# In three of a transformer kernel's linear layers, an input's high and low parts become one 512-column operand

## The chip, the cores and the metric

The kernel runs on one core of a Trainium2 chip. The metric is the device time of one execution, in microseconds (us). The version before takes 1366.85 us, the median of three runs (1366.1 to 1367.48).

## What is computed

The reference chains two transformer-like parts over 256 tokens of width 1024. The first has a mixer (pooling, indexed sparse attention, gates) and a convolved feed-forward layer. The second has two layers with a context stream of another 256 tokens. Cut to the three layers that the change touches:

```python
def hybrid_mixer(...):
    ...
    return merged @ w_out                      # "w_out": 1024 -> 1024

def conv_ffn(xn, w_up, conv_w, conv_b, w_down):
    ...
    return (jax.nn.silu(a) * b) @ w_down       # "w_down": 2816 -> 1024

def _mlp(h, w1, w2):
    return jnp.square(jax.nn.relu(h @ w1)) @ w2   # its last call: "w2_1", 4096 -> 1024
```

Each result is added to the running activation: h + hybrid_mixer(...), h + conv_ffn(...), and x + gx2 * _mlp(...). The whole is in float32.

## The kernel before

**Layout.** Features lie on the partitions and tokens along the columns. R holds the activation as 8 chunks of 128 features by 512 columns, tokens of x on the left (0 to 255), tokens of the context on the right.

**Precision.** A float32 product is made of float32r products of split operands. A weight is split into whi and wlo, an input into a high and a low part (Ahi and Alo, Hhi and Hlo, Zhi and Zlo). The product is whi·high + whi·low + wlo·high, all three summed in one PSUM bank.

**Blocks, units, chunks.** A weight matrix is cut into blocks of 128 x 128; 8 blocks are a unit, one DMA of 512 KB into one of 9 raw buffers. ScalarE writes whi for a unit (line 1000, 4 buffers), VectorE writes wlo over the raw buffer (line 1463). A chunk is one output tile of 128 features, summed over kt blocks: kt is 8 in w_out (8 chunks, 64 blocks), 22 in w_down (8 chunks, 176 blocks), 32 in w2_1 (8 chunks, 256 blocks). For a layer with only the tokens of x, a block costs three matmuls of 256 columns: whi with the high part (line 508), whi with the low part (line 520), wlo with the high part (line 522). Layers that also have the context do the same with 512 columns. The chunks take turns in three PSUM banks of 512 columns; of these the 256-column layers use the left half.

**First chunk of a layer with kt of 8.** Where n is 0 and the layer is not in EARLY, linear does the high parts of the eight blocks with whi and wlo (lines 508 and 511) first, and then the eight low parts (line 515), because the inputs are still being made. Of the three layers this is so in w_out alone.

**Reading.** VectorE adds a finished chunk to R: line 1714 in w_out, line 1780 in w_down, line 1857 (gated) in w2_1. The reading is queued between the wlo operations in the order that walk gives.

**What sets the order.** The order of units is PLAN, written out by weight_plan. In w_out and in w_up it places two units of another matrix (raw<-in_ada, eight matmuls at line 563) behind every second unit. SP's queue loads unit i when unit i-9 has been used. Each engine walks the same plan in a hand-written order. Waits are on semaphores; Waits.wait_ge leaves out one already met.

**Work around the change.** After w_out's chunks, ScalarE makes the input of w_up (line 1011) and squares of R (line 1015). TensorE sums the squares after w_up's first chunk (lines 611 and 613). In w_down, ScalarE and GpSimd sum the squares of the context (lines 1015 and 2094), and TensorE takes the sum after unit 4 (lines 611 and 613, called from after_down). After w_down's last chunk come two squares of R (line 1015), their sums over partitions on TensorE (lines 611 and 613), a reciprocal (line 1792), a root, and then ab_in's inputs. Its weights' first unit is loaded when w_down's unit 19 has been used, and its whi and wlo stand ahead of w_down's last reading in the queues of ScalarE and VectorE. w2_1 is the last layer: SP writes chunk c of R out (line 477) when VectorE has read it.

Of the kernel before, what the change touches and what calls it, by code (L numbers as in the profile page):

```python
# [262 lines left out]
def launch_program(nc, dram, out):  # L263
# [19 lines left out]
    R = sb("R", 8 * 512).rearrange("p (c t) -> p c t", c=8)  # L283
    Ahi = sb("Ahi", 8 * 512, f32r).rearrange("p (c t) -> p c t", c=8)
    Alo = sb("Alo", 8 * 512, f32r).rearrange("p (c t) -> p c t", c=8)
    h_at = here[0]
    here[0] += 65536
    Hhi = sb("Hhi", 8192, f32r, at=h_at)
    Hlo = sb("Hlo", 8192, f32r, at=h_at + 32768)
    par = sb("par", N_PARAMS)  # L290
# [45 lines left out]
    def h32(name, cols, at):  # L336
# [18 lines left out]
    z2 = h32("z2", 2048, 38912).rearrange("p (c t) -> p c t", c=8)  # L355
    Zhi, Zlo = [sb(f"Z{x}", 1024, f32r, at=h_at + 47104 + 4096 * i).rearrange("p (c t) -> p c t", c=4)
                for i, x in enumerate(("hi", "lo"))]
    F = h32("F", 2048, 0).rearrange("p (c t) -> p c t", c=4)
# [122 lines left out]
    def tensor_program(e):  # L481
        w = Waits(e)
        bank6 = [None]

        def linear(name, T, acts, hi_ready, lo_ready, during=None, following=None, midway=None, begin=0):


            kt, nt = WEIGHTS[name]
            for n in range(begin, nt):
# [6 lines left out]
                for k in range(kt):  # L496
# [9 lines left out]
                    w.wait_ge(S("whi"), s + 1)  # L506
                    hi_ready(k)
                    e.matmul(o, w_hi, ah, start=k == 0, stop=False)  # L508
                    if kt == 8 and n == 0 and name not in EARLY:
                        low_ready(s)  # L510
                        e.matmul(o, w_lo, ah, start=False, stop=False)
                        if last:
                            for x in range(8):
                                lo_ready(x)
                                m = e.matmul(o, whi[s % NHI][:, 128 * x:128 * x + 128], acts(x)[1][:, :Tn],
                                             start=False, stop=x == 7)
                            m.then_inc(S("mm").sem, 1)
# [255 lines left out]
        linear("w_pool", 256, lambda k: (Ahi[:, 4 + k], Alo[:, 4 + k]), ready("mix_hi"), ready("mix_lo"))  # L773
        linear("w_out", 256, z_parts, ready("Z_hi"), ready("Z_lo"), following=lambda u: ada_following("w_out", u))

# [12 lines left out]

        linear("w_down", 256, lambda k: Hc(k, 256), ready("H_hi"), ready("H_lo"), following=after_down)
        row_sum(ps[5][:, :256], ssum[:, :256], sq[0][:, :256], "nx_part", 6, "nx_sq", 8, "nx_sum")  # L790
# [195 lines left out]
        linear("w1_1", 258, lambda k: (Ehi[:, k], Elo[:, k]), e2_hi, e2_lo, during=during_1)  # L986
        linear("w2_1", 256, lambda k: Hc(k, 256), ready("h1_hi"), ready("h1_lo"))

# [465 lines left out]
    def vector_program(e):  # L1454
# [251 lines left out]
        for what, i in walk("w_out"):  # L1706
            if what == "unit":
                los(UNIT["w_out", i])
            if what == "chunk":
                if i:  # L1710
                    early_lo("e1", E_hi, E_lo, i - 1, LEFT, param("g_ffn", i - 1))
                o = product("w_out", i)[:, :256]

                e.scalar_tensor_tensor(R[:, i, LEFT], o, 0.5, R[:, i, LEFT], MUL, ADD).then_inc(S("wout_r").sem, 1)
                if i == 7:
                    w.wait_ge(S("wout_r"), 8)
                    early_lo("e1", E_hi, E_lo, 7, LEFT, param("g_ffn", 7))
# [57 lines left out]
        for what, i in walk("w_down"):  # L1775
            if what == "unit":
                los(UNIT["w_down", i])
            if what == "chunk":
                o = product("w_down", i)[:, :256]
                e.tensor_tensor(R[:, i, LEFT], o, R[:, i, LEFT], ADD).then_inc(S("down_r").sem, 1)  # L1780
            if what == "after":
# [288 lines left out]
        for what, i in walk("w2_1"):  # L2070
            if what == "unit":
                los(UNIT["w2_1", i])
            if what == "chunk":
                gated("w2_1", "d1_r", 1, 1, i, 256, None)

# [330 lines left out]
```

## Time and profile before

| | |
|---|---|
| median of 3 runs | 1366.85 us |
| profiled execution, its own time | 1367.44 us |
| its span, first to last instruction | 1365.2 us |
| granted TensorE clock over the span | 0.995 |
| w_out, TensorE, about | 191.9 to 220.5 us |
| w_down, TensorE | 356.7 to 422.4 us |
| w2_1, TensorE | 1270.1 to 1362.4 us |

A row of a timeline has its start from the beginning of the span, its duration and its instruction. Matmuls are pipelined, so one lasts longer in the rows than the distance between the starts of two: the distance is what a matmul costs in a stream. PE is TensorE's matmuls, PEld its weight loads, DVE VectorE, ACT ScalarE, POOL GpSimd, SPq the DMA queue of SyncE.

### The profile page before, as it was taken

The page shows a single profiled execution, that of the slowest core. Times are in us where ns is not written, and L with a number is a line of the kernel's source. Part 1 is how long each engine was busy: PE and PEld are TensorE (multiplying, and loading weights), DVE is VectorE, ACT ScalarE, POOL GpSimd, SP SyncE. Part 2 cuts the span into 40 slices and gives each one's busy share as a digit, 9 for nine tenths or more (in the row PEclk, how much of TensorE's full clock was granted, in tenths as well). Part 3 has the DMA queues.
Part 4 walks back from the last instruction along what each step waited for, and adds up shares of the span by engine and source line. Part 5 has one row for each costly group of instructions (what it writes and reads, how often), then busy time and mean ns, then how long its engine had stood idle before and what let it go on. Part 6 is the DMA issues. An engine that isn't in the chain of part 4 may idle for free.

```text
span 1365.2 us, 20841 instructions
## 1 busy us (share of the span) xinstructions
PE 1330.2 (97%) x8320; PEld 1141.9 (84%) x8320; DVE 810.3 (59%) x1223; ACT 594.2 (44%) x952; POOL 429.6 (31%) x439
## 2 busy tenths in 40 slices
PE   6999999999999999989999999999899999999999
PEld 6888898899997788858878888887577777999999
DVE  6678576899776452386633444343667765855443
ACT  4336545566664132244421244222545544666432
POOL 3443221222420003244400044111466552388200
PEclk9999999999999999999999999999999999999999
DMA  6777457865556231344534444444523221555552
GB/s 256 261 252 270 139 175 275 296 204 184 181 172 207 69 96 59 97 166 156 168 127 156 150 139 146 142 144 159 181 93 108 94 93 32 188 184 185 184 185 78
DMA packets 63967, 220.13 MB, mean 161 GB/s; under 512 B 6912, under 2 KB 10240, under 8 KB 63872
## 3 DMA queue, kind: packets, MB, share of 16 engines
q1 hardware_dynamic: 63584, 218.56, 47.9%
q8 instruction: 66, 1.08, 0.3%
q10 hardware_dynamic: 288, 0.25, 0.1%
q14 instruction: 29, 0.24, 0.1%
HBM read 217.73 MB, written 1.05 MB: 160 GB/s over the span
## 4 chain that ended last, share of the span: by engine, by line
PE 89%; DVE 6%; issue 2%; POOL 1%; ACT 1%; DMA 1%; DVEq 0%; ACTq 0%; POOLq 0%
PE ps L508 26%; PE ps L522 25%; PE ps L520 25%; PE ps L563 2%; PE ps L882 1%; DVE wlo L1463 1%; PE ps L909 1%; PE ps L896 1%; PE ps L828 1%; DVE Alo L1886 1%; DVE tmp L1901 1%; PE ps L875 1%; POOL ssum_c L2094 1%; DVE tmp L1728 1%; PE ps L807 0%
## 5 line engine op out<-in xcount | busy, mean ns | idle before, releaser
L508 PE MATMUL ps<-Ahi,whi 128*128 128x256 f32 (+2 forms) x1640 | 541.4, 330 | 8.3 <-ACT Ahi L1025 5.5
L522 PE MATMUL ps<-Ahi,wlo 128*128 128x256 f32 (+2 forms) x1596 | 510.2, 320 | 0.7 <-DVE wlo L1463 0.6
L520 PE MATMUL ps<-Alo,whi 128*128 128x256 f32 (+2 forms) x1596 | 509.8, 319 | 0.0
L1463 DVE TENSOR_TENSOR wlo<-raw,whi 128x1024 fp32r<-128x1024 f32 x305 | 388.2, 1277 | 104.0 <-ACT whi L1000 104.0
L1000 ACT ACTIVATE whi<-raw 128x1024 fp32r<-128x1024 f32 x305 | 320.1, 1051 | 284.4 <-PE ps L522 220.3
L508 PEld LDWEIGHTS ps<-Ahi,whi 128*128 128x128 f32 x1640 | 312.6, 191 | 73.4 <-issue 30.8
L522 PEld LDWEIGHTS ps<-Ahi,wlo 128*128 128x128 f32 x1596 | 304.5, 191 | 22.7 <-DVE wlo L1463 1.6
L520 PEld LDWEIGHTS ps<-Alo,whi 128*128 128x128 f32 x1596 | 304.5, 191 | 22.4 <-issue 1.7
L520 PE MATMUL ps<-Hlo,whi 128*128 128x256 f32 (+1 forms) x728 | 233.8, 321 | 0.0
L508 PE MATMUL ps<-Hhi,whi 128*128 128x256 f32 (+1 forms) x688 | 222.5, 323 | 0.0
L522 PE MATMUL ps<-Hhi,wlo 128*128 128x256 f32 (+1 forms) x688 | 221.9, 322 | 0.0
L520 PEld LDWEIGHTS ps<-Hlo,whi 128*128 128x128 f32 x728 | 139.3, 191 | 10.0
L2083 POOL TENSOR_TENSOR Hlo<-tmp,Hhi 128x256 fp32r<-128x256 f32 (+1 forms) x86 | 121.5, 1413 | 62.7 <-ACT Hhi L1295 40.8
L508 PEld LDWEIGHTS ps<-Hhi,whi 128*128 128x128 f32 x688 | 131.0, 190 | 11.6 <-issue 0.8
L522 PEld LDWEIGHTS ps<-Hhi,wlo 128*128 128x128 f32 x688 | 131.0, 190 | 10.0
L1857 DVE SCALAR_TENSOR_TENSOR R<-ps,ada,R 128x256 f32<-128x256 f32 x64 | 28.7, 480 | 156.0 <-PE ps L522 151.9
L2211 POOL TENSOR_TENSOR tmp<-tmp 128x512 f32<-128x512 f32 (+1 forms) x64 | 54.4, 850 | 166.3 <-ACT tmp L1290 166.3
L2094 POOL TENSOR_TENSOR ssum<-ssum,sq 128x256 f32<-128x256 f32 (+1 forms) x30 | 31.8, 1059 | 166.4 <-ACT sq L1015 166.4
L1541 DVE SCALAR_TENSOR_TENSOR modsum<-raw,cond,modsum 128x1024 f32<-128x1024 f32 x36 | 62.0, 1739 | 0.0
L1290 ACT ACTIVATE tmp<-ps 128x512 f32<-128x512 f32 x32 | 19.2, 599 | 97.5 <-PE ps L522 90.8
L1295 ACT ACTIVATE Hhi<-tmp 128x512 fp32r<-128x512 f32 (+1 forms) x64 | 33.7, 526 | 35.6 <-POOL tmp L2211 35.4
L2225 POOL TENSOR_TENSOR tmp<-tmp,tmp 128x512 f32<-128x512 f32 (+1 forms) x32 | 33.8, 1056 | 44.9 <-ACT tmp L1348 43.6
(263 smaller groups left out, 1286.0 us busy)
## 6 DMA issues: line engine op xcount, KB each, us to landing
raw<-in_ada SPq DMA_DIRECT2D x96, 512.0 KB, 4.3
raw<-in_w SPq DMA_DIRECT2D x64, 512.0 KB, 3.5
raw<-in_w_up SPq DMA_DIRECT2D x44, 512.0 KB, 3.9
raw<-in_w_in SPq DMA_DIRECT2D x38, 512.0 KB, 5.1
raw<-in_w_0a SPq DMA_DIRECT2D x32, 512.0 KB, 3.6
raw<-in_w_0b SPq DMA_DIRECT2D x32, 512.0 KB, 3.5
raw<-in_na_in SPq DMA_DIRECT2D x24, 512.0 KB, 5.6
raw<-in_w_down SPq DMA_DIRECT2D x22, 512.0 KB, 3.5
```

The costliest lines, as they stand in the source:

```text
L508: e.matmul(o, w_hi, ah, start=k == 0, stop=False)
L520: e.matmul(o, w_hi, al, start=False, stop=False)
L522: m = e.matmul(o, w_lo, ah, start=False, stop=last)
L1000: e.activation(whi[s % NHI][:, :cols], raw[i % NRAW][:, :cols], ACT.Copy).then_inc(S("whi").sem, 1)
L1295: e.activation(Hc(n, T)[0], tmp[n % 5][:, :T], ACT.Copy).then_inc(S(st + "_hi").sem, 1)
L1463: e.tensor_tensor(wlo[i % NRAW][:, :cols], raw[i % NRAW][:, :cols], plain(whi[s % NHI][:, :cols]), SUB).then_inc(S("wlo").sem, 1)
L1541: d = e.scalar_tensor_tensor(total, raw[i % NRAW], cond[:, k, v:v + 1], total, MUL, ADD)
L1857: e.scalar_tensor_tensor(R[:, n, half(q)], o[:, half(q)], gate, R[:, n, half(q)], MUL, ADD).then_inc(S(made).sem, 1)
L2083: e.tensor_tensor(into, x, plain(hi), SUB).then_inc(S(done).sem, 1)
L2094: e.tensor_tensor(total, total, x, ADD).then_inc(S(st + "_part").sem, 1)
L2211: e.tensor_tensor(x, x, x, MUL).then_inc(S(st + "_sq").sem, 1)
L2225: e.tensor_tensor(m, m, r, MUL).then_inc(own.sem, own.up())
```

## The change

In the three layers the high and the low part of an input are put into one tile each (A, H and Z), so that one access pattern (A2, H2, Z2) gives 256 columns of the high part and 256 of the low part of a chunk. whi then meets both in one matmul of 512 columns, which fills the whole bank: whi·high on the left and whi·low on the right. wlo·high is added on the left, as before. The wait for the low part stands ahead of this matmul. VectorE adds the left half of the bank to R and then, after a wait for that, the right half. The first chunk of w_out keeps its order and puts the low parts' sum on the right.

```diff
-    Ahi = sb("Ahi", 8 * 512, f32r).rearrange("p (c t) -> p c t", c=8)
-    Alo = sb("Alo", 8 * 512, f32r).rearrange("p (c t) -> p c t", c=8)
+    A = sb("A", 2 * 8 * 512, f32r).rearrange("p (x c t) -> p x c t", x=2, c=8)
+    Ahi, Alo, A2 = A[:, 0], A[:, 1], A.rearrange("p x c t -> p c x t")[:, :, :, 0:256]
...
-    Hhi = sb("Hhi", 8192, f32r, at=h_at)
-    Hlo = sb("Hlo", 8192, f32r, at=h_at + 32768)
+    H = sb("H", 2 * 8192, f32r, at=h_at)
+    Hhi, Hlo, H2 = H[:, 0:8192], H[:, 8192:16384], H.rearrange("p (x c t) -> p c x t", x=2, t=256)
...
-    Zhi, Zlo = [sb(f"Z{x}", 1024, f32r, at=h_at + 47104 + 4096 * i).rearrange("p (c t) -> p c t", c=4)
-                for i, x in enumerate(("hi", "lo"))]
+    Z = sb("Z", 2 * 1024, f32r, at=h_at + 47104).rearrange("p (x c t) -> p x c t", x=2, c=4)
+    Zhi, Zlo, Z2 = Z[:, 0], Z[:, 1], Z.rearrange("p x c t -> p c x t")
...
                     hi_ready(k)
+                    if both and not (kt == 8 and n == 0):
+                        lo_ready(k)
+                        e.matmul(ps[g % 3].rearrange("p (x t) -> p x t", x=2), w_hi, both(k), start=k == 0, stop=False)
+                        low_ready(s)
+                        m = e.matmul(o, w_lo, ah, start=False, stop=last)
+                        if last or end:
+                            m.then_inc(S("mm").sem, 1)
...
+                        continue
                     e.matmul(o, w_hi, ah, start=k == 0, stop=False)
...
-                                m = e.matmul(o, whi[s % NHI][:, 128 * x:128 * x + 128], acts(x)[1][:, :Tn],
-                                             start=False, stop=x == 7)
+                                m = e.matmul(ps[g % 3][:, 256:512] if both else o, whi[s % NHI][:, 128 * x:128 * x + 128],
+                                             acts(x)[1][:, :Tn], start=False, stop=x == 7)
...
-        linear("w_out", 256, z_parts, ready("Z_hi"), ready("Z_lo"), following=lambda u: ada_following("w_out", u))
+        linear("w_out", 256, z_parts, ready("Z_hi"), ready("Z_lo"), following=lambda u: ada_following("w_out", u),
+               both=lambda k: A2[:, k] if k < 4 else Z2[:, k - 4])
...
-        linear("w_down", 256, lambda k: Hc(k, 256), ready("H_hi"), ready("H_lo"), following=after_down)
+        linear("w_down", 256, lambda k: Hc(k, 256), ready("H_hi"), ready("H_lo"), following=after_down, both=lambda k: H2[:, k])
...
-        linear("w2_1", 256, lambda k: Hc(k, 256), ready("h1_hi"), ready("h1_lo"))
+        linear("w2_1", 256, lambda k: Hc(k, 256), ready("h1_hi"), ready("h1_lo"), both=lambda k: H2[:, k])
...
-                o = product("w_out", i)[:, :256]
-
-                e.scalar_tensor_tensor(R[:, i, LEFT], o, 0.5, R[:, i, LEFT], MUL, ADD).then_inc(S("wout_r").sem, 1)
+                o = product("w_out", i)
+
+                e.scalar_tensor_tensor(R[:, i, LEFT], o[:, LEFT], 0.5, R[:, i, LEFT], MUL, ADD).then_inc(own.sem, own.up())
+                w.wait_ge(own, own.n)
+                e.scalar_tensor_tensor(R[:, i, LEFT], o[:, RIGHT], 0.5, R[:, i, LEFT], MUL, ADD).then_inc(S("wout_r").sem, 1)
```

The readings of w_down (tensor_tensor) and w2_1 (scalar_tensor_tensor with the gate, in place of the call of gated) are doubled in the same way, with the wait between the two halves.

## Rows read from the trace of the kernel before

**Rows 1.** The page: span, busy time of each engine, the chain that ended last.

```profile
span 1365.2 us, 20841 instructions
...
PE 1330.2 (97%) x8320; PEld 1141.9 (84%) x8320; DVE 810.3 (59%) x1223; ACT 594.2 (44%) x952; POOL 429.6 (31%) x439
...
PE 89%; DVE 6%; issue 2%; POOL 1%; ACT 1%; DMA 1%; DVEq 0%; ACTq 0%; POOLq 0%
```

**Rows 2.** Busy time of each engine, granted clock and DMA by stretch.

```profile
core 0: us, PE busy (x) PEld busy (x) DVE busy (x) ACT busy (x) POOL busy (x), PEclk, DMA share, GB/s
1270.00:1362.00 92.00, 92.00 (x770) 92.00 (x769) 39.17 (x39) 31.92 (x32) 3.29 (x4) 1.00 0.47 150
604.00:685.00 81.00, 81.00 (x358) 66.88 (x357) 52.81 (x36) 31.89 (x44) 39.24 (x30) 1.00 0.48 163
373.00:416.00 43.00, 43.00 (x358) 42.95 (x357) 27.88 (x38) 23.44 (x36) 9.77 (x11) 1.00 0.55 175
196.00:222.00 26.00, 25.52 (x206) 21.62 (x206) 15.11 (x22) 14.11 (x24) 5.00 (x7) 1.00 0.76 266
```

**Rows 3.** Timeline, w2_1: its first matmul and its last instructions.

```profile
1270.09 0.28 PE L508 MATMUL ps<-Hhi,whi 128*128 128x256 f32 x1
...
1362.11 0.28 PE L522 MATMUL ps<-Hhi,wlo 128*128 128x256 f32 x1
1362.43 0.48 DVE L1857 SCALAR_TENSOR_TENSOR R<-ps,ada,R 128x256 f32<-128x256 f32 x1 [8.77 <-PE ps L522]
1362.94 0.33 SPq L477 DMA_DIRECT2D out_y<-R  x1
```

**Rows 4.** Timeline, a stream of 512-column matmuls, its first and last.

```profile
604.10 0.39 PE L508 MATMUL ps<-Ahi,whi 128*128 128x512 f32 x1
...
684.82 0.39 PE L522 MATMUL ps<-Ahi,wlo 128*128 128x512 f32 x1
```

**Rows 5.** Timeline, weight loads beside matmuls, 512 columns and 256 columns.

```profile
700.31 0.39 PE L520 MATMUL ps<-Hlo,whi 128*128 128x512 f32 x1
700.54 0.39 PE L522 MATMUL ps<-Hhi,wlo 128*128 128x512 f32 x1
...
700.31 0.19 PEld L522 LDWEIGHTS ps<-Hhi,wlo 128*128 128x128 f32 x1
...
1361.87 0.28 PE L508 MATMUL ps<-Hhi,whi 128*128 128x256 f32 x1
1361.87 0.19 PEld L520 LDWEIGHTS ps<-Hlo,whi 128*128 128x128 f32 x1
1361.99 0.28 PE L520 MATMUL ps<-Hlo,whi 128*128 128x256 f32 x1
```

**Rows 6.** Timeline, w_down: its first matmul, and around the sum after unit 4.

```profile
356.67 0.28 PE L508 MATMUL ps<-Hhi,whi 128*128 128x256 f32 x1
...
370.95 0.28 PE L522 MATMUL ps<-Hhi,wlo 128*128 128x256 f32 x1
372.45 0.70 PE L611 MATMUL ps<-ssum_c,con 128*128 128x256 f32 x2 [1.22 <-POOL ssum_c L2094]
372.99 0.59 PE L613 MATMUL ps<-X,con 128*128 128x256 f32 x2
373.23 0.47 PE L508 MATMUL ps<-Hhi,whi 128*128 128x256 f32 x1
```

**Rows 7.** GpSimd in w_down: its last Hlo (timeline), the sum of squares (the chain).

```profile
361.81 0.75 POOL L2083 TENSOR_TENSOR Hlo<-tmp,Hhi 128x256 fp32r<-128x256 f32 x1 [0.59 <-ACT Hhi L1165]
...
364.26 1.36 POOL ssum_c L2094
...
365.75 1.55 POOL ssum_c L2094
...
369.11 0.75 POOL ssum_c L2094
...
370.88 1.53 POOL ssum_c L2094
```

**Rows 8.** The end of w_down: TensorE's last matmul (timeline), the chain that ended last.

```profile
422.25 0.28 PE L522 MATMUL ps<-Hhi,wlo 128*128 128x256 f32 x1
...
416.81 3.45 DMA raw<-in_ab_in
...
420.28 1.07 ACT whi L1000
...
421.37 1.22 DVE wlo L1463
422.59 0.41 DVE R L1780
...
423.03 0.42 ACT sq L1015
...
423.50 0.70 PE ps L613 x2
```

**Rows 9.** Timeline, VectorE, two pairs of operations with a wait of its own between.

```profile
358.41 0.48 DVE L1728 SCALAR_TENSOR_TENSOR tmp<-Y,par,tmp 128x255 f32<-128x255 f32 x1 [0.74 <-ACT tmp L1187]
358.93 0.48 DVE L1730 SCALAR_TENSOR_TENSOR tmp<-Y,par,tmp 128x254 f32<-128x254 f32 x1
...
425.18 0.42 DVE L1790 SCALAR_TENSOR_TENSOR X<-ps,X 128x256 f32<-128x256 f32 x1 [0.52 <-PE ps L613]
425.63 1.75 DVE L1792 RECIPROCAL X<-X 128x256 f32<-128x256 f32 x1
```

**Rows 10.** Timeline, the end of w_out: ScalarE, and TensorE's sum after w_up's first chunk.

```profile
221.41 0.51 ACT L1011 ACTIVATE Ahi<-R,par 128x256 fp32r<-128x256 f32 x1 [0.58 <-DVE R L1714]
221.83 1.04 ACT L1000 ACTIVATE whi<-raw 128x1024 fp32r<-128x1024 f32 x1
222.78 0.40 ACT L1015 ACTIVATE sq<-R 128x256 f32<-128x256 f32 x1
...
224.48 0.59 PE L611 MATMUL ps<-ssum,con 128*128 128x256 f32 x2
224.91 0.59 PE L613 MATMUL ps<-sq,con 128*128 128x256 f32 x2
```

**Rows 11.** Timeline, VectorE: four pieces of 256 columns, against one run of 1024.

```profile
5.38 1.22 DVE L1553 TENSOR_TENSOR squares<-R 128x1024 f32<-128x1024 f32 x1 [5.38 <-DMA R<-in_x]
...
421.37 1.22 DVE L1463 TENSOR_TENSOR wlo<-raw,whi 128x1024 fp32r<-128x1024 f32 x1 [5.16 <-ACT whi L1000]
```

More of the change, by code:

```diff
@@ L483, in tensor_program, with linear @@
         bank6 = [None]
-        def linear(name, T, acts, hi_ready, lo_ready, during=None, following=None, midway=None, begin=0):
+        def linear(name, T, acts, hi_ready, lo_ready, during=None, following=None, midway=None, begin=0,
+                   both=None):
             kt, nt = WEIGHTS[name]
@@ L507, in linear @@
                     hi_ready(k)
+                    if both and not (kt == 8 and n == 0):
[5 more added lines that the diff above has]
+                            m.then_inc(S("mm").sem, 1)
+                        if last and during:
+                            during(n)
+                        if end and following:
+                            following(blk // 8)
+                        continue
                     e.matmul(o, w_hi, ah, start=k == 0, stop=False)
@@ L1778, in vector_program @@
             if what == "chunk":
-                o = product("w_down", i)[:, :256]
-                e.tensor_tensor(R[:, i, LEFT], o, R[:, i, LEFT], ADD).then_inc(S("down_r").sem, 1)
+                o = product("w_down", i)
+                e.tensor_tensor(R[:, i, LEFT], o[:, LEFT], R[:, i, LEFT], ADD).then_inc(own.sem, own.up())
+                w.wait_ge(own, own.n)
+                e.tensor_tensor(R[:, i, LEFT], o[:, RIGHT], R[:, i, LEFT], ADD).then_inc(S("down_r").sem, 1)
             if what == "after":
@@ L2073, in vector_program @@
             if what == "chunk":
-                gated("w2_1", "d1_r", 1, 1, i, 256, None)
+                o, gate = product("w2_1", i), ada[:, 1, 0, 40 + i:41 + i]
+                e.scalar_tensor_tensor(R[:, i, LEFT], o[:, LEFT], gate, R[:, i, LEFT], MUL, ADD).then_inc(own.sem, own.up())
+                w.wait_ge(own, own.n)
+                e.scalar_tensor_tensor(R[:, i, LEFT], o[:, RIGHT], gate, R[:, i, LEFT], MUL, ADD).then_inc(S("d1_r").sem, 1)
     def gpsimd_program(e):
```

## The prediction

> **What bounds the kernel now.** I read the page first [rows 1]. TensorE's matmuls are busy for 1330.2 of 1365.2 us and carry 89% of the chain that ended last, so a saving counts only if it shortens TensorE's own stream, or a wait between its matmuls. The table by stretch [rows 2] shows that in all three layers TensorE is busy almost without a gap at the full granted clock (1.00, 2.4 GHz), VectorE for 39.17 of 92 us in w2_1 and 27.88 of 43 in w_down, and the DMA for 0.47 to 0.76 of the time. So the question is what one matmul costs inside a stream.
>
> That is the distance between starts, not the duration in a row. w2_1 has 8 x 32 x 3 = 768 matmuls of 256 columns; from the first to the last start [rows 3] are 92.02 us and 767 steps, **119.97 ns each**. The 512-column stream [rows 4] goes from the second block of a chunk to the last of w1_0a, 119 blocks of three, 80.72 us over 356 steps, **226.74 ns each**. The difference, 106.8 ns for 256 columns, is 2.4 columns per ns. Each matmul thus pays some 13.3 ns above its columns, at either width. It pays with every matmul, so fewer and wider ones are cheaper.
>
> **TensorE's part.** A block was three narrow matmuls, 3 x 119.97 = 359.9 ns. It becomes one wide and one narrow, 226.74 + 119.97 = 346.7 ns: 13.2 ns less. No row has the two widths taking turns, so the pair's cost is put together. The weight loads support it: the load for the next matmul starts when the one before it starts, at both widths [rows 5]. In the new stream the load that belongs to the next wide matmul can start with the narrow one and has its 120 ns as now, and the other load has 227. The blocks concerned are 56 in w_out (its first chunk keeps its order), 176 in w_down and 256 in w2_1, 488 in all. Raw savings: 56 x 13.2 = 0.74, 176 x 13.2 = 2.33, 256 x 13.2 = 3.39; 6.46 us.
>
> Here the Trainium skill (TensorE: Matmul & The Clock Gate, "Back-to-back issue gap") gives N / 2.4 + 2.5 ns for a warm stream. By that the estimate would be 2.5 ns saved per block, 1.2 us in all. The two rows say 13.3 at either width, and the sum goes by them.
>
> The wide operand is two pieces of 256 columns, 16 or 32 KB apart in the partition. TensorE reads no such operand in a row. The nearest row is VectorE's: four pieces of R take 1.22 us, like one run of 1024 columns [rows 11]. I take nothing for the jump. As bounds: a restart could cost as much as one matmul's excess, 13.3 ns, and more if it stalls; on the other side, the excess of the narrow matmul might vanish beside a wide one, another 13.3 saved.
>
> **Where it is lost.** In w_down TensorE waits after unit 4 for GpSimd's sum of the context's squares [rows 6]. It had the 40 blocks done at 356.67 + 40 x 0.36 = 371.07 and went on at 372.45. GpSimd's chain [rows 7] is tied to the end of w_up, not to w_down, so the 40 blocks' 0.53 us only lengthen this wait. GpSimd's operations last 0.75 us alone and 1.4 to 1.55 beside VectorE's; the doubled reading of chunk 0 moves a wlo operation by half a us there, which may hurt or help by up to 0.8 us. I take 0.
>
> At the end of w_down, the load of ab_in's first unit starts when unit 19 is done (416.81), then come whi, wlo, and only then VectorE's last reading at 422.59 [rows 8]. TensorE's last product is ready at about the same moment: its last matmul begins at 422.25 [rows 8], and readings start 0.32 after that, as 1362.11 and 1362.43 show [rows 3]. The two chains are now level. The last 16 blocks' 0.21 us are therefore lost to the load. 176 - 40 - 16 = 120 blocks are left, 1.59 us.
>
> **What VectorE adds.** Two operations with a wait between them start 0.52 apart where one lasts 0.48, and 0.45 where it lasts 0.42 [rows 9]. Within a layer this is hidden: a chunk's reading has two more chunks of TensorE's work before its bank is wanted, and VectorE has room. Eight more readings of 0.52 in w2_1 are 4.2 us against 53 idle [rows 2]; w_out's VectorE is busy for 15.11 of 26 us and takes 3.7 more. At a layer's end it shows:
> - w_out: the last chunk's input for w_up is ready at 221.92 and its square at 223.18; the sum wants it at 224.9 [rows 10]. TensorE is 0.74 earlier and the reading 0.45 later relative to it. Cover 1.7 us, used 0.45: nothing.
> - w_down: the reading stands on the chain to ScalarE's squares and the sums [rows 8]: 0.45 us. What is late next is ab_in's input, by the same.
> - w2_1: the last reading precedes the last output transfer [rows 3]: 0.52 us.
>
> **Waits, queues, memory.** The low part is now awaited one matmul sooner. In w_down GpSimd's last Hlo (block 21) is made by 362.6 [rows 7] and wanted at 356.67 + 21 x 0.35 = 364.0; in w2_1 block 31 comes 10.7 us after the first. Behind this wait stands only TensorE's own stream. No DMA is added or moved. SP's loads are freed by TensorE's progress and come 4% closer together, 266 to some 275 GB/s in w_out, at a DMA share of 0.76 now. The tiles occupy the same room.
>
> **The sum.** 0.74 + (1.59 - 0.45) + (3.39 - 0.52) = **4.75 us**. The profiled execution took 1367.44 us, 2.2 more than its span and 0.6 more than the median; the difference is taken from the median: 1366.85 - 4.75 = **1362.1 us**, 0.35% less.
>
> **The rivals.**
> 1. *The jump costs a restart.* If a second piece of an operand costs what a second matmul does, the wide one takes 240 ns and a block is unchanged. Only the two tails remain: 1366.85 + 0.97 = 1367.8 us, no change. For it: no row of TensorE excludes it. Against it: VectorE's equal times [rows 11]. Chance 0.10.
> 2. *The jump stalls, slower than before.* Its place is the wide matmul in 488 blocks. It decides from 17 ns per jump: (17 - 13.2) x 488 = 1.8 us, with the tails 2.8. At twice the excess, 26.6 ns, 6.5 + 0.97 us are added, 1374.3 us. For it speaks nothing in the rows, against it the same row as above. Chance 0.06. Here the Trainium skill (PSUM — Partial Sum Buffer, "Specifications (TRN2)") says that any non-contiguous access pattern slows matmuls significantly, without a figure. In the bank the halves lie side by side, so it would have to hold for the operand read; no row shows it.
> 3. *The narrow matmul's excess is its weight load.* The narrow stream has its loads busy for 92.00 of 92 us, the wide one for 66.88 of 81 [rows 2]. If a load could begin during the wide matmul for both of its successors, a block would save up to 26.5 ns. The 432 blocks that count would give 5.7 us more, 1356.4 us. Against it: the load starts with the matmul just before its own [rows 5]. Chance 0.05.
> 4. *The excess is mostly not per matmul.* If only 2.5 ns are saved per block, 432 x 2.5 = 1.1 us meet tails of 0.97 us: 1366.7 us. The two rows' equal excess speaks against it. Chance 0.04. That is the Trainium skill's gap rule from above, which the trace does not bear out.
> 5. *The change does not do what it says*, for one if the two pieces were fetched as two matmuls: the number of matmuls would stay 8320, and the time with it. It comes out as rival 1 and is counted there.
>
> **How the numbers follow.** My forecast has 0.75; its own range, by GpSimd's 0.8 us either way and a jump of up to 3 ns (1.3 us), is 1361 to 1364.5. The range leaves out rival 2, rival 1's full price and most of rival 3 (together under 0.2), takes in rival 4 and half the restart's price, and is 1360.2 to 1366.8. A measurement of this kernel can tell about 0.2%, 2.7 us, from no change. Faster by more than that: forecast and rival 3, 0.80. Within it: rivals 1 and 4 and little else, 0.14. Slower: rival 2, 0.06.
>
> **What would show it.** TensorE has 488 matmuls fewer, 7832. In w2_1, 512 starts span 256 x 0.3467 = 88.8 us, against 92.0. A wide matmul's start to the next is 227 ns, a narrow one's 120. The wait for GpSimd after unit 4 grows from 1.22 us to about 1.75. The last sum of w_down still follows a chain from the load of ab_in, with two readings of 0.42. The last output transfer starts about 1.0 us after the last product. The forecast is wrong if wide matmuls are more than 230 ns apart, if the narrow ones fall under 115, or if new waits for wlo stand in TensorE's stream.

## The result and the profile after

The changed kernel takes 1364.24 us in the median of 20 runs (1361.73 to 1366.55), the kernel before 1366.49 us in 20 runs beside it (1364.81 to 1367.99). The ratio is **0.9985, 95% interval 0.9978 to 0.9992**: 2.25 us faster, between 1.1 and 3.0. The direction is as forecast and the time lies in the range; the gain is half of the 4.75 us of the sum. The profiled execution took 1364.33 us.

The page after, for [rows 1]:

```profile
span 1362.1 us, 19938 instructions
...
PE 1325.6 (97%) x7832; PEld 1114.5 (82%) x7832; DVE 821.2 (60%) x1247; ACT 594.1 (44%) x952; POOL 428.5 (31%) x439
...
PE 88%; DVE 7%; issue 2%; DMA 1%; ACT 1%; POOL 1%; DVEq 0%; ACTq 0%; SPq 0%; POOLq 0%
```

488 matmuls are gone, as forecast, and TensorE still carries the chain. The table by stretch, for [rows 2]: w2_1, then w_down behind its fifth unit.

```profile
core 0: us, PE busy (x) PEld busy (x) DVE busy (x) ACT busy (x) POOL busy (x), PEclk, DMA share, GB/s
1268.00:1358.00 90.00, 90.00 (x512) 78.11 (x511) 42.56 (x46) 31.87 (x32) 3.33 (x4) 1.00 0.46 152
373.00:414.00 41.00, 41.00 (x238) 35.86 (x237) 30.09 (x44) 23.04 (x35) 8.55 (x11) 1.00 0.55 175
```

TensorE is still busy without a gap, at the full clock. w2_1 needs 90 us for its 512 matmuls where 88.8 were forecast. The start of each layer's first `wlo` matmul shows where the time went (us, before and after, shift; each from the timeline):

```
w_out, its second chunk    196.96    196.14   -0.82
w_up, first chunk          221.84    220.55   -1.29
w_down, first chunk        356.91    355.97   -0.94
w_down, end of unit 4      370.95    369.75   -1.20
w_down, end of unit 19     416.49    414.24   -2.25
w_down, last matmul        422.25    419.79   -2.46
ab_in                      429.45    427.49   -1.96
w2_1, first chunk         1270.32   1268.36   -1.96
w2_1, last matmul         1362.11   1358.46   -3.65
last transfer of out_y    1362.94   1359.80   -3.14
```

The first 0.82 us are not the change's: they arise before w_out's second chunk, where both kernels have the same matmuls. Until 160 us the profile of before was 0.67 us ahead; in the next 12 us, in which it has a lower granted clock, it fell back by 1.49. Before, then after:

```profile
160.00:172.00 12.00, 10.02 (x67) 9.45 (x66) 6.35 (x10) 6.46 (x13) 3.15 (x4) 0.86 0.46 133
```

```profile
160.00:172.00 12.00, 10.02 (x80) 9.44 (x79) 7.12 (x13) 7.08 (x14) 3.15 (x4) 1.00 0.41 138
```

From there on the sum of the prediction and the trace compare as follows (gains positive):

```
                              forecast   measured
w_out                            0.74       0.47
wait at w_up's first chunk       0         -0.35
w_down, to the end of unit 19    1.59       1.31
from there to ab_in             -0.45      -0.29
w2_1                             3.39       1.69
last reading                    -0.52      -0.51
sum                              4.75       2.32
```

2.32 us from one pair of traces, 2.25 from the medians. (The last 16 blocks of w_down, behind unit 19, gained another 0.21 us, and ab_in's load took them back, as forecast.) Two terms are well off, w2_1 and the wait in w_up; w_out and w_down are off by less. Each can be seen.

**w2_1: the rhythm.** The timeline of TensorE in w2_1 after:

```profile
1299.56 0.40 PE L513 MATMUL ps<-H,whi 128*128 128x512 f32 x1
1299.80 0.28 PE L515 MATMUL ps<-H,wlo 128*128 128x256 f32 x1
1299.92 0.40 PE L513 MATMUL ps<-H,whi 128*128 128x512 f32 x1
...
1300.62 0.40 PE L513 MATMUL ps<-H,whi 128*128 128x512 f32 x1
```

And in w_down, behind the wait after unit 4:

```profile
379.69 0.39 PE L513 MATMUL ps<-H,whi 128*128 128x512 f32 x1
...
380.73 0.40 PE L513 MATMUL ps<-H,whi 128*128 128x512 f32 x1
```

Three blocks take 1.06 us in the first and 1.04 us in the second. The trace's nanoseconds show two patterns. In the first the distances (wide to narrow plus narrow to wide) repeat every three blocks: 242+119, 236+114, 232+117 ns. In the second they repeat every two: 231+113, 232+117. Over long stretches a block takes **353.3 ns** in the first (w2_1, 90.10 us for 255 blocks from its first `wlo` matmul to its last) and **346.7 ns** in the second (w_down, 41.26 us for the 119 from unit 5 to unit 19); the expectations below call them 353.6 and 346.5. The forecast was 346.7, and before the change it was 360.0 (91.79 us in w2_1). All of w2_1 and the first five units of w_down run in the longer rhythm, the rest of w_down in the shorter one.

**w_up: a new wait.** TensorE at the end of w_up's first chunk, after:

```profile
222.82 0.28 PE L523 MATMUL ps<-A,whi 128*128 128x256 f32 x1
223.20 0.39 PE L535 MATMUL ps<-A,whi 128*128 128x256 f32 x1
```

VectorE at that place:

```profile
221.13 0.42 DVE L1730 SCALAR_TENSOR_TENSOR R<-ps,R 128x256 f32<-128x256 f32 x1
221.58 0.42 DVE L1732 SCALAR_TENSOR_TENSOR R<-ps,R 128x256 f32<-128x256 f32 x1
222.66 0.49 DVE L1492 SCALAR_TENSOR_TENSOR A<-R,par,A 128x256 fp32r<-128x256 f32 x1 [0.66 <-ACT A L1027]
```

The low part of w_up's last input (L1492) lasts from 222.66 to 223.15. TensorE wanted it at 222.94, 0.12 behind the start before, and started at 223.20; its next matmul (223.42) came 0.22 behind that one instead of 0.12. Together that is 0.36 us.

Before the change the same low part was ready at 222.53 and wanted at 224.24, 1.7 us of room; now it is 0.2 us late. Both traces show where the 1.9 us went. ScalarE makes the whi of w_up's first unit when its load has landed, before and after:

```profile
214.34 1.06 ACT L1000 ACTIVATE whi<-raw 128x1024 fp32r<-128x1024 f32 x1 [3.99 <-DMA raw<-in_w_up]
```

```profile
214.11 1.06 ACT L1016 ACTIVATE whi<-raw 128x1024 fp32r<-128x1024 f32 x1 [3.54 <-DMA raw<-in_w_up]
```

From there ScalarE and VectorE hand the work to each other up to this low part, for 8.19 us before and 9.03 after; several doubled readings stand in VectorE's part of it (L1730, L1732 are the last pair), and they cost some 0.85. The load itself took 7.00 us from its issue (207.09) to its landing instead of 6.22 (from 208.09), another 0.78. The last 0.3 us are TensorE's own gain, which was larger than that of the load's issue.

**The wait after unit 4** of w_down, for [rows 6]:

```profile
369.75 0.28 PE L515 MATMUL ps<-H,wlo 128*128 128x256 f32 x1
371.79 0.70 PE L626 MATMUL ps<-ssum_c,con 128*128 128x256 f32 x2 [1.76 <-POOL ssum_c L2117]
```

1.22 us became 1.76, the number of the forecast, but from other parts: the 40 blocks saved 0.26 us and not 0.53 (370.95 - 356.91 before, 369.75 - 355.97 after), and GpSimd's sum came 0.28 later, counted from w_down's start, because one of its additions lasted 1.79 us instead of 1.54. The end of w_down, in the chain that ended last, for [rows 8]:

```profile
414.55 3.36 DMA raw<-in_ab_in
...
417.93 1.07 ACT whi L1016
...
419.03 1.23 DVE wlo L1479
420.25 0.34 DVE R L1798
...
420.62 0.43 DVE R L1800
...
421.08 0.42 ACT sq L1031
```

The two readings stand one behind the other on that chain. So they do at the end of w2_1, for [rows 3]:

```profile
1358.46 0.28 PE L515 MATMUL ps<-H,wlo 128*128 128x256 f32 x1
1358.77 0.48 DVE L2095 SCALAR_TENSOR_TENSOR R<-ps,ada,R 128x256 f32<-128x256 f32 x1 [8.04 <-PE ps L515]
1359.29 0.48 DVE L2097 SCALAR_TENSOR_TENSOR R<-ps,ada,R 128x256 f32<-128x256 f32 x1
1359.80 0.33 SPq L478 DMA_DIRECT2D out_y<-R  x1
```

### The profile page after: what moved, and what is told of

It is laid out like the page before. It is cut to its first block, busy times and chain, and to the rows that moved or that the text cites. A ratio compares the mean times of both kernels' runs of the same rounds, so it can differ in the third digit from the quotient of the medians.

```text
span 1362.1 us, 19938 instructions
## 1 busy us (share of the span) xinstructions
PE 1325.6 (97%) x7832; PEld 1114.5 (82%) x7832; DVE 821.2 (60%) x1247; ACT 594.1 (44%) x952; POOL 428.5 (31%) x439
## 4 chain that ended last, share of the span: by engine, by line
PE 88%; DVE 7%; issue 2%; DMA 1%; ACT 1%; POOL 1%; DVEq 0%; ACTq 0%; SPq 0%; POOLq 0%
PE ps L523 22%; PE ps L537 22%; PE ps L535 22%; PE ps L513 7%; PE ps L515 3%; PE ps L578 2%; PE ps L898 1%; DVE wlo L1479 1%; PE ps L925 1%; PE ps L912 1%; PE ps L844 1%; DVE A L1906 1%; DVE tmp L1921 1%; PE ps L891 1%; POOL ssum_c L2117 1%
## 5 line engine op out<-in xcount | busy, mean ns | idle before, releaser
L523 PE MATMUL ps<-A,whi 128*128 128x256 f32 (+2 forms) x1612 | 533.4, 331 | 8.1 <-ACT A L1041 5.5
L537 PE MATMUL ps<-A,wlo 128*128 128x256 f32 (+2 forms) x1568 | 502.4, 320 | 0.7 <-DVE wlo L1479 0.6
L535 PE MATMUL ps<-A,whi 128*128 128x256 f32 (+2 forms) x1568 | 502.1, 320 | 0.1
L523 PEld LDWEIGHTS ps<-A,whi 128*128 128x128 f32 x1612 | 307.0, 190 | 70.7 <-issue 29.1
L537 PEld LDWEIGHTS ps<-A,wlo 128*128 128x128 f32 x1568 | 299.0, 191 | 22.7 <-DVE wlo L1479 1.6
L535 PEld LDWEIGHTS ps<-A,whi 128*128 128x128 f32 x1568 | 299.0, 191 | 22.7 <-issue 1.7
L513 PE MATMUL ps<-H,whi 128*128 128x512 f32 x432 | 152.1, 398 | 0.0
L2106 POOL TENSOR_TENSOR H<-tmp,H 128x256 fp32r<-128x256 f32 (+1 forms) x86 | 120.6, 1402 | 60.0 <-ACT H L1311 40.8
L515 PE MATMUL ps<-H,wlo 128*128 128x256 f32 x432 | 120.9, 280 | 0.0
L523 PE MATMUL ps<-H,whi 128*128 128x512 f32 (+1 forms) x296 | 112.2, 379 | 0.0
L535 PE MATMUL ps<-H,whi 128*128 128x512 f32 (+1 forms) x296 | 111.7, 377 | 0.0
L513 PEld LDWEIGHTS ps<-H,whi 128*128 128x128 f32 x432 | 81.2, 188 | 19.7
L515 PEld LDWEIGHTS ps<-H,wlo 128*128 128x128 f32 x432 | 81.6, 189 | 0.0
L523 PEld LDWEIGHTS ps<-H,whi 128*128 128x128 f32 x296 | 56.5, 191 | 11.7 <-issue 0.8
L537 PEld LDWEIGHTS ps<-H,wlo 128*128 128x128 f32 x296 | 56.5, 191 | 10.8 <-DVE wlo L1479 0.8
L535 PEld LDWEIGHTS ps<-H,whi 128*128 128x128 f32 x296 | 56.5, 191 | 9.9
```

Of the source, the lines that this page charges most:

```text
L513: e.matmul(ps[g % 3].rearrange("p (x t) -> p x t", x=2), w_hi, both(k), start=k == 0, stop=False)
L515: m = e.matmul(o, w_lo, ah, start=False, stop=last)
L535: e.matmul(o, w_hi, al, start=False, stop=False)
L537: m = e.matmul(o, w_lo, ah, start=False, stop=last)
L2106: e.tensor_tensor(into, x, plain(hi), SUB).then_inc(S(done).sem, 1)
```

## The experiments

Each ratio is against the kernel before on the same chip. The kernels beside each other in a group share those runs: group 1 (e) 1366.91 us, group 2 (f) 1366.05, group 3 (g) 1366.53 in the median.

**e1, the two pieces of the operand side by side.** The changed kernel, with the high and low part of a chunk adjacent in H and Z, so that the wide operand is one run of 512 columns (A keeps its layout).

```diff
+        if T == 256:
+            return H2[:, c, 0], H2[:, c, 1]
...
-    Hhi, Hlo, H2 = ..., H.rearrange("p (x c t) -> p c x t", x=2, t=256)
+    Hhi, Hlo, H2 = ..., H.rearrange("p (c x t) -> p c x t", x=2, t=256)
```

> The changed kernel with the two pieces of the wide operand side by side: H as (chunk, high/low, 256) for w_down and w2_1, Z likewise; A, in w_out's first four blocks, keeps its jump. In the changed kernel a block (one wide and one narrow matmul) took either 346.5 ns (after unit 4 of w_down) or 353.6 ns (w2_1 and before unit 4). Theory J, the jump between the pieces costs it: every block of w_down and w2_1 now takes 346.7 ns, w2_1's 256 blocks span 88.8 us in place of 90.1, and the time falls by about 1.7 us against the changed kernel. Theory R, two widths taking turns fall into one of two rhythms wherever the pieces lie: 353.6 is seen again in some stretch, and the time is the changed kernel's within 1 us.

Measured: 1365.18 us (11 runs), ratio 0.9988 [0.9979, 0.9997]. From the first `wlo` matmul of w2_1 (1267.79) to its last (1357.89) are 90.10 us, the changed kernel's time to the hundredth. Its timeline has the same rhythm, three blocks in 1.07 us (the first wide matmul and the third one behind it):

```profile
1299.70 0.40 PE L515 MATMUL ps<-H,whi 128*128 128x512 f32 x1
...
1300.77 0.40 PE L515 MATMUL ps<-H,whi 128*128 128x512 f32 x1
```

The distance between the pieces costs nothing, and the missing 1.7 us of w2_1 are not its price. The Trainium skill (PSUM — Partial Sum Buffer, "Specifications (TRN2)") says that non-contiguous patterns slow matmuls significantly. It says so in its row on the cache lines of PSUM, and the bank is written without a gap in both kernels, so for the bank no run tests it; for the operand that is read, two pieces of 256 columns are as fast as one run (90.10 us both).

**e2, the same readings and layout, but two narrow matmuls.** The wide matmul is undone, the two products still go to the two halves of the bank.

```diff
-    e.matmul(ps[g % 3].rearrange("p (x t) -> p x t", x=2), w_hi, both(k), ...)
+    e.matmul(o, w_hi, ah, start=k == 0, stop=False)
+    e.matmul(ps[g % 3][:, 256:512], w_hi, al, start=False, stop=False)
```

> The changed kernel with its wide matmul put back as two narrow ones, one into each half of the bank; the doubled readings and the new layout stay. It measures what VectorE's second readings cost alone. My theory: 0.45 us at the end of w_down and 0.52 at the end of w2_1, and no wait in w_up, as TensorE is no earlier there: 0.97 us above the version before, 1367.5; blocks of 360 ns. Rival: the readings are hidden everywhere but at the very end, +0.5 us. Rival: the new layout costs a matmul something as well, blocks above 360 ns and more than 1.5 us above.

Measured: 1368.72 us (11 runs), ratio 1.0015 [1.0006, 1.0024], slower by 1.8 us (0.8 to 3.3) where 0.97 was worked out. No wait stands in w_up, as expected. w2_1's stream takes 91.79 us, as before the change, so halves instead of one target cost TensorE nothing. The readings cost 0.46 us between w_down and ab_in and 0.52 at the end:

```profile
1362.60 0.28 PE L516 MATMUL ps<-H,wlo 128*128 128x256 f32 x1
...
1363.95 0.33 SPq L478 DMA_DIRECT2D out_y<-R  x1
```

The wait after unit 4, 1.22 us in the kernel before, is 1.47: one of GpSimd's additions lasts 1.78 us instead of 1.54, as in the changed kernel, where the doubled reading stands too. These three terms are 1.2 us. Against this kernel the changed one is 3.5 us faster (1365.19 in e4, same runs of before), which is about what the wide matmul alone is worth; part of it, and of the 0.6 us that e2 is above the three terms, may be the clock: 8 of e2's 11 runs have a mean granted clock of 0.995 or less, 4 of 11 in e4 and 5 of 33 in the kernel before.

**e3, two wide, then two narrow.** Each pair of blocks issues its two wide matmuls and then its two narrow ones; the sums are the same up to their order.

```diff
+    if k % 2:
+        continue
...
     e.matmul(o2, w_hi, both(k), start=k == 0, stop=False)
+    e.matmul(o2, w_hi2, both(k + 1), start=False, stop=False)
     e.matmul(o, w_lo, ah, start=False, stop=False)
+    m = e.matmul(o, w_lo2, acts(k + 1)[0][:, :Tn], start=False, stop=last)
```

> The changed kernel with its matmuls ordered by twos: two wide ones, then the two narrow ones of the same two blocks. Work, layout and readings are unchanged. Theory R (widths taking turns make the slower rhythm): the rhythm changes; two blocks take 693 ns everywhere, w2_1 spans 88.8 us. Theory J (the jump): the wide matmuls are as irregular as before, and w2_1 spans about 90.1 us.

Measured: 1363.15 us (10 runs), ratio 0.9976 [0.9967, 0.9985]. In w2_1:

```profile
1268.55 0.28 PE L521 MATMUL ps<-H,wlo 128*128 128x256 f32 x1
...
1356.57 0.40 PE L518 MATMUL ps<-H,whi 128*128 128x512 f32 x1
1356.80 0.40 PE L519 MATMUL ps<-H,whi 128*128 128x512 f32 x1
1357.03 0.28 PE L521 MATMUL ps<-H,wlo 128*128 128x256 f32 x1
1357.15 0.27 PE L523 MATMUL ps<-H,wlo 128*128 128x256 f32 x1
```

From 1268.55 to 1357.15 are 88.60 us for 254 blocks and one narrow matmul, (88.60 - 0.12) / 254 = 348.3 ns a block, against 353.3. The same operands, widths and loads, in another order, are 5 ns cheaper: the longer rhythm belongs to widths that take turns one by one. Two blocks take 696.7 ns, though, and not the 693 of the expectation; the order by twos has a price of its own, the same in w_down and w2_1 and in all five profiles of kernels that have it (e3, f3, g3, f4, g4).

**e4, the changed kernel again.**

> The changed kernel once more, for a second profile. If the two rhythms (346.5 and 353.6 ns a block) depend on the phase in which a stretch begins, w2_1 may come out at 88.7 us (fast) or 90.1 us (slow) here, and the times of single executions scatter over some 3 us, more than those of the version before. If the rhythm belongs to the layer, w2_1 spans 90.1 us again and w_down from unit 5 on has 346.5 ns a block.

Measured: 1365.19 us (11 runs), ratio 0.9985 [0.9976, 0.9994], the first result once more. w2_1 takes 90.10 us again (1266.39 to 1356.49). w_down again starts long and turns short behind the wait. So far this is what was expected if the rhythm belongs to the layer. But the second pair of w_out's units, long in the first trace (2.83 us for 8 blocks), was short here (2.78). The same code can have either rhythm.

**f1, a nudge ahead of each unit of w2_1.** A short extra matmul into bank 3, of 8 columns ahead of unit 0 and 8 more ahead of each next one, up to 256.

```diff
+    if name == "w2_1" and blk % 8 == 0:
+        e.matmul(ps[3][:, :8 * (blk // 8 + 1)], w_hi, ah[:, :8 * (blk // 8 + 1)], start=True, stop=True)
```

> The changed kernel with one extra short matmul ahead of each of w2_1's 32 units, into an unused bank, 8 columns wide before the first unit and 8 more before each next one. It shifts the phase in which the stream of wide and narrow matmuls starts. If the rhythm (346.5 or 353.6 ns a block) is set by that phase, units of both kinds are seen within w2_1: 8 blocks in 2.77 or in 2.83 us. If it belongs to the layer, all 32 are alike.

Measured: one time, 1366.18 us. Both rhythms now stand within w2_1, each from nudge to nudge: 18 units are short and 14 long, the first seven short, then in irregular turns. Behind the nudges of 56 and of 64 columns (the nudge, a wide matmul, the third wide one behind it):

```profile
1284.67 0.19 PE L514 MATMUL ps<-H,whi 128*128 128x56 f32 x1
...
1285.13 0.40 PE L515 MATMUL ps<-H,whi 128*128 128x512 f32 x1
...
1286.17 0.39 PE L515 MATMUL ps<-H,whi 128*128 128x512 f32 x1
```

```profile
1287.56 0.19 PE L514 MATMUL ps<-H,whi 128*128 128x64 f32 x1
...
1288.02 0.40 PE L515 MATMUL ps<-H,whi 128*128 128x512 f32 x1
...
1289.08 0.40 PE L515 MATMUL ps<-H,whi 128*128 128x512 f32 x1
```

Three blocks take 1.04 us behind the first and 1.06 behind the second, at the same clock, with the same instructions. What differs is the width of the nudge, and with it the moment at which the stretch starts. That it is the moment is the likelier reading, since wider nudges give now one rhythm, now the other, and e4 has both from the same code; no run parts the two. Nothing between the nudges brings it out of the rhythm in which it began.

**f2, the last chunk of each layer as before.** The last chunk has three narrow matmuls and one reading, the others are changed (their right half is now read first). The part of the diff on TensorE:

```diff
-    if both and not (kt == 8 and n == 0):
+    if both and n < nt - 1 and not (kt == 8 and n == 0):
```

> The changed kernel, but the last chunk of each of the three layers goes by three narrow matmuls a block and one reading, as before the change. Where the second reading stands on the path it is gone: at the end of w_down from the last matmul to ab_in 0.45 us less, at the end of w2_1 0.52 less, and TensorE's wait in w_up's first chunk for the low part of chunk 7 (0.36 us from start to start in the changed kernel) is gone. The last chunks' matmuls cost some of it back: 22 and 32 blocks of 7 to 13 ns, 0.2 to 0.4 us each, in w_down mostly hidden behind ab_in's load. Together 0.5 to 0.9 us below the changed kernel. Rival: w_up's wait comes from the load of w_up's weights and not from the readings, then it stays.

Measured: 1363.29 us (11 runs), ratio 0.9982 [0.9973, 0.9991]. In w_up the wait is gone; the matmuls that were 0.38 apart are 0.12 apart:

```profile
223.84 0.28 PE L523 MATMUL ps<-A,whi 128*128 128x256 f32 x1
223.96 0.28 PE L535 MATMUL ps<-A,whi 128*128 128x256 f32 x1
```

But the single reading isn't what decided it. The way from the whi of w_up's first unit to this low part is 0.45 us shorter with one reading fewer, 8.57 to 8.59 us in the five profiles with narrow last chunks (f2, f3, g3, f4, g4) against 9.03 or 9.04 in the changed kernel, e1, e3, e4, f1 and g1. Yet g1 and f1, which up to here run the changed kernel's code, don't wait either (0.74 and 0.16 us of room), and f4, with the single reading, still is 0.06 us late. What differs is the load of w_up's first unit: from issue to landing it took 5.95 us here, 6.05 in g1, 6.62 in f1, 7.00 in the changed kernel's profile, 7.07 in e4, 7.20 in e1, 7.35 in f4. So the rival of the expectation, the load, is the larger part of it; why the load's time varies no run shows.

At the end:

```profile
1360.68 0.28 PE L537 MATMUL ps<-H,wlo 128*128 128x256 f32 x1
...
1361.51 0.33 SPq L478 DMA_DIRECT2D out_y<-R  x1
```

One reading is left, and the last transfer starts 0.83 us behind the last matmul instead of 1.34. The price is a narrow chunk of 32 blocks in w2_1, 32 x 6.6 = 0.2 us in the long rhythm. The median is below the changed kernel's ratio by 0.0003, which the intervals can't tell from nothing; the traces show the piece at the end, the times don't.

**f3 and g3, pairs and the last chunk narrow.** e3 and f2 together.

> Matmuls ordered by twos (two wide, two narrow) and the last chunk of each layer narrow with one reading. If both effects are what I take them for, they add up: the order by twos was measured at 1363.2, less 0.5 to 0.8 for the readings: 1362.5, 4.3 us (0.32%) below the version before.

Measured: 1364.08 us (11 runs), ratio 0.9985 [0.9976, 0.9994], a miss: not better than either part. Its timeline after unit 4:

```profile
369.04 0.28 PE L523 MATMUL ps<-H,wlo 128*128 128x256 f32 x1
371.32 0.98 PE L634 MATMUL ps<-ssum_c,con 128*128 128x256 f32 x2 [1.99 <-POOL ssum_c L2128]
```

and the stretch behind it, in the columns of the first table:

```profile
371.30:374.70 3.40, 3.38 (x10) 2.75 (x11) 0.00 (x0) 0.40 (x1) 0.00 (x0) 0.54 0.26 106
```

TensorE had idled for 1.99 us; behind that the granted clock is 0.54, nearly all of the stretch at 1.2 GHz, and 10 matmuls stand in 3.4 us. So I asked whether that was the cause, and ran the same kernel once more.

> The kernel with matmuls by twos and narrow last chunks, for a second profile. In the first, TensorE waited 2.28 us from start to start after unit 4, and its granted clock fell to half for 3.4 us at 371.6. If that comes from the length of the wait, it is seen again here: a granted clock below 1 in the stretch from 371 to 376 us, and a first wide matmul after the sum spaced 0.8 us. If it was chance, the clock is 1.00 there and the span about 1.7 us shorter.

Measured: one time, 1359.89 us. The wait is as long, 1.99 us for the sum (from the matmul at 368.69 to the one at 370.96), but the clock is not lower. The same stretch:

```profile
371.30:374.70 3.40, 3.40 (x20) 2.97 (x19) 1.14 (x3) 0.04 (x1) 0.00 (x0) 1.00 0.21 84
```

The expectation that it would be seen again failed: the lower clock is no fixed follower of this wait. The span is 3.6 us shorter than f3's, where 1.7 was expected for this case. Of the 3.6 us, 1.64 arise behind the wait (368 to 376 us) and 1.40 between 1150 and 1170, where f3 has a second stretch of lower clock (0.83 from 1156 to 1166, against 1.00 in g3). How often either came in f3's timed runs, and so what held f3's median at 1364, stays open.

**f4 and g4, the same and the sum of squares one unit later.** The wait for GpSimd is taken away by asking for its sum after unit 5.

```diff
-            if u == 4:
+            if u == 5:
                 row_sum(ps[4][:, :256], ssum_c, ...)
```

> The same, and TensorE takes the sum of the context's squares after unit 5 of w_down, not after unit 4. If the wait after unit 4 (about 2.0 us from start to start in the changed kernel) swallows what the first 40 blocks save, it goes: GpSimd's sum is done before unit 5 ends, w_down's first six units run without a gap, 1.5 to 1.9 us less: 1360.8. Rival: something behind the sum, the root and the norm of the context, becomes late and the time stays.

Measured: 1359.71 us (5 runs), ratio 0.9956 [0.9943, 0.997], a microsecond below the 1360.8 worked out; the rival falls. And again, beside g1 and g2:

> Matmuls by twos, narrow last chunks and the sum after unit 5, once more with five rounds: 0.9956 of the version before is expected again, within 0.001, and no mean clock below 0.996.

Measured: 1359.2 us (5 runs), ratio 0.9954 [0.9941, 0.9966]. The mean clocks of the five are 0.996 three times, 0.995 and 0.992, so that part of the expectation missed; the time held.

**g1, the changed kernel with the later sum alone.**

> The changed kernel, and the sum of the context's squares is taken after unit 5 of w_down. In the changed kernel's profile TensorE waited 2.04 us there from start to start, 1.92 above a matmul's spacing. That goes, and what the first 40 blocks save (0.3 to 0.5 us) now counts. If the longer wait also lets TensorE's granted clock fall in some executions, the median falls by more than the profile's 1.9 us: 2.2 to 2.8 us below the changed kernel, about 1362 beside a version before of 1366.5, and hardly an execution has a mean clock of 0.995 or less. If the clock plays no part, 1.9 us.

Measured: 1362.32 us (6 runs), ratio 0.997 [0.9958, 0.9981]. The sum starts at 372.66, 0.11 us behind the matmul before it: no wait is left. Against the changed kernel's ratio this is 0.15%, 2.0 us, between the 1.9 and the 2.2 to 2.8 of the two theories, and 2 of the 6 runs have a mean clock of 0.995 or less; the run doesn't decide between them. Its trace shows something else. From the first to the last `wlo` matmul of w_down it is 1.12 us shorter than the changed kernel's (62.69 against 63.82), not 1.9, because behind the sum w_down stays in the long rhythm:

```profile
379.52 0.40 PE L513 MATMUL ps<-H,whi 128*128 128x512 f32 x1
...
380.58 0.40 PE L513 MATMUL ps<-H,whi 128*128 128x512 f32 x1
```

Three blocks take 1.06 us here and 1.04 at the same place of the changed kernel, and it is so to the layer's end: 136 blocks at 6.6 ns, 0.9 us.

**g2, the kernel before with the later sum alone.**

> The version before, with the sum after unit 5 of w_down and nothing else. Its wait was 1.50 us from start to start, so 1.4 us less, 0.10%. The difference of the run above to this one is what the change is worth where its first 40 blocks count: 3 to 4.9 us, by the rhythm that w_down and w2_1 fall into. Rival: the gain of the run above comes from unit 5 alone and this one gains as much.

Measured: 1364.52 us (11 runs), ratio 0.9988 [0.9978, 0.9997]; its trace is 1.49 us ahead in w_down. Beside it g1 is 2.2 us faster, less than the 3 us expected. That this equals the 2.25 us with the wait doesn't mean that the wait hid nothing: without it the first 40 blocks' gain counts, but the 0.9 us of the long rhythm behind the sum are lost. Of the gain of f4, g1 and g4, 2.0 us in the medians (0.4 to 3.0 by g2's interval) are the later sum's, to be had without the change.

The version that beats both kernels is g4, 0.46% under the kernel before: 4.6 to 8.1 us by the interval, 7.3 by the medians of group 3. Of these 7.3 the medians give 2.0 to the later sum (g2), 2.2 more to the change (g1), and 3.1 to the pairs and the narrow last chunk (g4); the intervals of g1 and g2 overlap slightly, so the shares are rough.

## Why the prediction was half right

- **"The number of matmuls falls by 488, and a matmul costs 13.3 ns above its columns."** Held. In the short rhythm a block is 346.7 ns, as put together, and w_down's 120 blocks that count gave 1.58 of 1.59 us.
- **"226.74 + 119.97 = 346.7 ns", for every block.** This is the step that failed: the price of the pair was right in one of two rhythms, and the mis-sized term of the sum is **w2_1, 3.39 us, which measured 1.69**. The prediction said itself that no row has the two widths taking turns, and it bounded the pair by the jump and by the load, up to 13 ns either way. The true value of 353.3 lay between those bounds but had another cause: e1 excludes the jump, e3 shows that the order of widths makes it, and e4 and f1 that the same stream can start in either rhythm. Nothing here shows what in TensorE keeps it. w_out's 0.47 for 0.74 is the same error, since part of its units ran in the long rhythm. That the forecast's own range, 1361 to 1364.5, still held the time is luck: it comes from allowances, of up to 3 ns for a jump that costs nothing and of 0.8 us for GpSimd. The prediction's own signs of being wrong were there: in w2_1 a wide matmul's start to the next is 236.6 ns in the mean, above the 230 named, and even in the short rhythm it is 231.8 and the narrow one's 114.8, under 115. Only the sum of the two is right in the short rhythm, not the two prices. New waits for wlo, the third sign, are not in the trace.
- **"w_out: cover 1.7 us, used 0.45: nothing."** Failed, and in the use, not in the cover. 1.7 us were there before, at the square [rows 10] and at the low part that VectorE makes beside it. The use was 1.9 us: the prediction counted the last chunk's reading alone, where several doubled readings lie on the way from the load of w_up's first unit (0.85), and took the load's own time as fixed, where it was 0.78 longer. The wait of 0.36 us is no fixed price either: none in g1 and f1, 0.34 of idle and 0.10 behind it in e4.
- **"w_down … the 40 blocks' 0.53 us only lengthen this wait."** The wait came out at 1.76 us for 1.75, which is luck: the 40 blocks saved 0.26, in the long rhythm, and GpSimd's sum lost 0.28, which was put at 0 within 0.8. In the sum this is the 0.28 us by which w_down misses its 1.59; its 120 blocks behind the wait gave 1.58.
- **"The two chains are now level" and the readings' 0.45 us.** The mechanism held: the load of 3.36 us first and both readings on the chain, and the last 16 blocks' gain lost to the load. From unit 19's end to ab_in 0.29 us were lost and not 0.45: the load was 0.09 shorter than before, and from the start of wlo to the square the chain took 2.05 us instead of 1.66, 0.39 more.
- **"w2_1: the last reading", 0.52 us.** Held: 0.52 in e2, 0.51 in the changed kernel; f2 gets it back.
- **The rivals.** Restart and stall of the jump fall with e1. The load's rival (26.5 ns a block) falls, since no rhythm is under 346. "Only 2.5 ns saved per block" would have been 0.6 us in w2_1 where 1.69 was seen in the long rhythm and 13 ns a block in the short one; the gap rule of the Trainium skill (TensorE: Matmul & The Clock Gate, "Back-to-back issue gap"), N / 2.4 + 2.5 ns, is not borne out by either. (The section gives the rule for a matmul by itself; the page has the same figure for warm back-to-back matmuls in another place.) The doing-something-else rival falls with the count, 7832.

Open: why the rhythm is kept, why w2_1 itself began in the long one in every profile in which the widths take turns without nudges (the changed kernel, e1, e4, f2, g1), and why f3's timed runs lie 4 us above its second kernel's single one. The changed kernel's runs also spread over 4.8 us, the kernel before's over 3.2, and 12 of its 20 have a mean clock of 0.995 or less. The two profiles of the changed kernel show a part of it: between 1156 and 1166 us the first has a granted clock of 0.83 and the second (e4) of 1.00, and the first loses 1.5 us there. What brings such a stretch in one run and not in the next wasn't isolated.

## What to carry to other kernels

Where matmuls stream without a gap, each one fewer is worth its fixed excess, but the price of a mix of widths has to be measured as a mix, not added up from two pure streams: issue equal widths together. When readings are doubled, count all of those that lie between a load and the operation that needs it, not only the last one, and ask how much the load's own time varies: here 4.99 to 7.35 us for the same load. The last chunk of the last layer has no work behind it to hide a second reading; in its old form it starts the output 0.5 us sooner in the trace (f2), though the times don't show it. And before a wait is removed, ask what it did besides costing time: here the stream that started anew behind it ran in the cheaper rhythm.

## What the runs showed of the hardware

A stream in which a matmul of 512 columns and one of 256 take turns has at least two steady rhythms, 346.7 and 353.3 ns a pair at the same full clock, kept for up to 256 pairs. The same code fell into either (w_out's units 2 and 3 in the changed kernel and in e4), and which one seems to hang on the moment of the start (f1). A two-and-two order gives 348.3 ns. An operand of two pieces 32 KB apart streams as fast as one run (90.10 us both). The load of one 512 KB unit, at the same place of the program, took 4.99 (e2) to 7.35 us (f4) from issue to landing in the fourteen profiles of this case. And an idle stretch of TensorE of 1.99 us was followed in one execution by 1.2 GHz (granted clock 0.54 over 3.4 us, 10 matmuls), and in another of the same kernel by the full clock (20 matmuls).
